# Attention scores and values in 64x64 tiles of TensorE, and the transposes moved behind a projection product

## The chip, the cores and the metric

The kernel runs on one core of one Trainium2 chip. A core has five engines with their own instruction queues: TensorE (PE, with its weight loads as PEld), VectorE (DVE), ScalarE (ACT), GpSimd (POOL) and SyncE (SP), which here only issues DMAs. They meet through semaphores. The metric is the device time of one execution in microseconds (us), the median of several runs.

## What is computed

Two layers over a sequence of 1024 rows of width 1024: an attention layer and a state-space layer, each followed by a residual and a layer norm. The change is in the attention layer alone. It has 16 heads of 64 columns and three groups of dilation (1, 4, 16). In each group a query sees keys within a window; the three results are merged by their softmax denominators.

```python
def _dilated_attention_mixer(h, w_in, w_out):
    proj = h @ w_in
    qkv = proj[..., :N_DIL * 3 * A_WIDTH].reshape(bsz, s, N_DIL, 3, A_HEADS, A_HEAD_DIM)
    gate = proj[..., N_DIL * 3 * A_WIDTH:]
    for g, (window, dil) in enumerate(((128, 1), (512, 4), (2048, 16))):
        o, l = _dilated_group(qkv[:, :, g, 0], qkv[:, :, g, 1], qkv[:, :, g, 2], window, dil, slopes)
    ...
    wts = softmax(stack(lses)); o = einsum('bshg,bshgd->bshd', wts, stack(outs))
    return (o.reshape(bsz, s, A_WIDTH) * silu(gate)) @ w_out
```

A group computes scores, adds a bias that falls with the distance, takes the exponential of the difference to the maximum, and multiplies with the values.

## The kernel before

The attention layer takes about the first 1,100 us. It works on two heads at a time, eight pairs in all; all pairs but the last run through the same code, the last has an order of its own (`last_pair`). The projections of a pair are ten tiles of 128 output columns, taken two at a time by a scheme with seven block products instead of eight. I call these products 0 to 6 of a unit. A product is 12 matmuls of 128x512 in `product` (L687) with weights w_f, the forms. There are seven forms a unit. ScalarE rounds each (`round_form`, L1046) and GpSimd subtracts to get its low part (`low_part`, L576). Product i can only begin when the low part of form i is there (w_ready). For forms 3 and 4 GpSimd must work in this order: raw form 3 (L605), low part 3, a difference (L608), raw form 4 (L612), low part 4.

The attention of a pair is cut into ten steps, d = 0 to 9: four of group 0, four of group 1 and two of group 2. A step has two units of `prob`, one for each head. An even step stands before products 0 to 3 and an odd step before products 4 to 6 of the same unit (`pair`, `stretch`, L944). In step d TensorE does

- the transposes of the probabilities of step d (`transpose_probs`, L766) into two banks of tp, which DVE copies to probT (`copy_t`, L1404),
- the values of step d-1 (`values`, L829 and L840) into the bank op, which ScalarE copies to num,
- in steps 0, 3 and 8 the transposes of V (L775), also through tp, and here the transposes of the probabilities stand behind the scores,
- the scores of step d+1 (`scores`, L756) into two banks of sp_.

DVE then takes the maxima of the scores with the bias (`tops`, L1384), ScalarE the exponentials (`softmax`, L1107). On ScalarE the softmax of step d+1 stands, in an even step, between the rounding of forms 2 and 3 (`even_step`). A product of float32 operands shows two records in the trace for each matmul of the program. Scores take 64 rows (a head) by 128 queries of the array, two heads beside each other; values 128 keys by 64 columns, again two beside each other.

The banks of tp are taken in turn by a list of events (`t_events`); an event can begin when the event two places before it has been copied (t_free). At the end of a pair, in step 9, the statistics (mz, the maxima and denominators) are transposed (L788) beside the sums for the next layer's constants (L782). DVE copies them to st, SP writes them to memory and reads them back as cz, and DVE computes differences (L1482 to L1485) and shares (L1491 to L1495) from them in the next step 0.

## Time and profile before

| | us |
|---|---|
| median of 3 runs | 2021.14 |
| lowest, highest | 2020.3, 2025.38 |
| the profiled execution | 2021.59 |
| its span | 2019.8 |
| TensorE busy | 1971.7 |
| GpSimd busy | 1267.8 |
| DVE busy | 1331.6 |
| ScalarE busy | 1060.8 |

The span is what the profile covers of the profiled execution, 1.8 us less than its time. Matmuls overlap, so the length of a matmul record says less than the distance of its start to the next one's. Where an engine sits idle, the profile says in brackets for how long and who ended it.

### The profile page before, as it was taken

To read this page: it belongs to the slowest core of one execution; us is meant where nothing else is said; L and a number is where in the kernel's file an instruction comes from. 1 tells how busy PE (TensorE), PEld (TensorE's weight loads), DVE (VectorE), ACT (ScalarE), POOL (GpSimd) and SP (SyncE) were. 2 spreads that over 40 slices of the span, in tenths; PEclk is the share of its full clock that TensorE was granted. 3 is DMA by queue.
4 is the path that set the end of the run, shared out by engine and by line. 5 is a ranking of instruction groups with operands and counts; after the bars stand their busy time and mean duration, and the time that the engine had idled before them with its cause. 6 is when DMAs were issued, how large, how long until landed. Compare 5 with 4: busy or idle time off the path is not lost.

```text
span 2019.8 us, 30446 instructions
## 1 busy us (share of the span) xinstructions
PE 1971.7 (98%) x10759; PEld 1569.4 (78%) x10759; DVE 1331.6 (66%) x2595; ACT 1060.8 (53%) x2578; POOL 1267.8 (63%) x841
## 2 busy tenths in 40 slices
PE   7999999999999999999999999899999999999998
PEld 4888877878888788777777867687787787777887
DVE  7547566475575664756647676798598598497553
ACT  5455455555545555545555254765665675675320
POOL 0566775867768667686584445376576576586572
PEclk8999999999999999999999999999999999999999
DMA  9112232222213222123234523465365365377531
GB/s 302 46 58 59 76 94 56 79 68 76 84 55 94 75 66 79 60 74 104 56 97 163 163 104 65 150 177 161 116 178 157 120 178 157 120 198 233 174 125 42
DMA packets 117590, 229.27 MB, mean 114 GB/s; under 512 B 22464, under 2 KB 55872, under 8 KB 117440
## 3 DMA queue, kind: packets, MB, share of 16 engines
q1 hardware_dynamic: 117440, 227.32, 37.2%
q8 instruction: 87, 1.43, 0.3%
q14 instruction: 63, 0.52, 0.1%
HBM read 199.42 MB, written 27.86 MB: 113 GB/s over the span
## 4 chain that ended last, share of the span: by engine, by line
PE 79%; DVE 9%; issue 3%; ACT 3%; POOL 2%; DMA 2%; SPq 2%; DVEq 0%; POOLq 0%; ACTq 0%
PE pp L687 27%; PE pp_s L2542 15%; PE po L687 10%; PE sp_ L756 4%; PE tp L766 4%; PE po L840 2%; DVE stage_s L3222 2%; PE pp_s L2746 2%; PE yo_p L2746 2%; PE po L829 2%; PE st_p L2559 1%; PE st_p L2746 1%; PE fill L2746 1%; DVE vv L3143 1%; PE yo_p L2574 1%
## 5 line engine op out<-in xcount | busy, mean ns | idle before, releaser
L687 PE MATMUL pp<-h_forms_hi,w_f 128*128 128x512 f32 x1576 | 516.7, 396 | 4.1 <-DVE temps L1432 2.6
L687 PEld LDWEIGHTS pp<-h_forms_hi,w_f 128*128 128x128 f32 x1576 | 296.2, 188 | 78.4 <-issue 12.0
L687 PE MATMUL pp<-h_forms_lo,w_f 128*128 128x512 f32 x788 | 307.6, 390 | 0.0
L576 POOL TENSOR_TENSOR w_f<-w_raw,w_f 128x512 fp32r<-128x512 f32 x154 | 199.3, 1314 | 161.4 <-ACT w_f L1046 161.4
L2542 PE MATMUL pp_s<-h_hi,w_hi_s 128*128 128x512 f32 x624 | 269.5, 432 | 5.3 <-DVE stage_s L3222 2.7
L1107 ACT ACTIVATE prob<-prob,mz 128x256 f32<-128x256 f32 (+2 forms) x384 | 169.9, 444 | 157.2 <-DVE mz L1384 157.0
L2542 PE MATMUL pp_s<-h_hi,w_lo_s 128*128 128x512 f32 x624 | 245.1, 393 | 0.0
L2542 PE MATMUL pp_s<-h_lo,w_hi_s 128*128 128x512 f32 x624 | 244.3, 391 | 0.0
L576 POOL TENSOR_TENSOR w_f<-w_f_raw,w_f 128x512 fp32r<-128x512 f32 x117 | 151.2, 1292 | 95.5 <-ACT w_f L1046 95.5
L687 PE MATMUL po<-h_forms_hi,w_f 128*128 128x512 f32 x632 | 209.4, 391 | 0.0
L687 PEld LDWEIGHTS pp<-h_forms_lo,w_f 128*128 128x128 f32 x788 | 148.3, 188 | 28.5
L2542 PEld LDWEIGHTS pp_s<-h_hi,w_hi_s 128*128 128x128 f32 x624 | 117.6, 188 | 48.9 <-issue 18.3
L3222 DVE SCALAR_TENSOR_TENSOR stage_s<-pp_s,gconv,stage_s 128x512 f32<-128x512 f32 (+2 forms) x184 | 137.9, 749 | 26.1 <-ACT stage_s L2816 20.6
L1046 ACT ACTIVATE w_f<-w_f_raw 128x512 fp32r<-128x512 f32 x118 | 74.4, 631 | 137.6 <-POOL w_f_raw L612 99.6
L2542 PEld LDWEIGHTS pp_s<-h_lo,w_hi_s 128*128 128x128 f32 x624 | 117.7, 189 | 31.2 <-issue 10.1
L2439 POOL TENSOR_TENSOR vv<-rw,vv 128x1024 f32<-128x1024 f32 x32 | 76.8, 2400 | 101.3 <-DVE vv L3143 98.6
L687 PEld LDWEIGHTS po<-h_forms_hi,w_f 128*128 128x128 f32 x632 | 118.9, 188 | 26.4 <-issue 1.8
L2141 POOL TENSOR_TENSOR w_lo_s<-w_raw_s,w_hi_s 128x1024 fp32r<-128x1024 f32 x40 | 100.0, 2500 | 62.3 <-ACT w_hi_s L2151 62.2
L2542 PEld LDWEIGHTS pp_s<-h_hi,w_lo_s 128*128 128x128 f32 x624 | 117.5, 188 | 26.3
L1384 DVE CUSTOM_DVE_ANT_0 prob<-sp_,bias,slope 128x256 f32<-128x256 f32 (+2 forms) x384 | 134.3, 406 | 3.9 <-PE sp_ L756 2.4
L1404 DVE COPY probT<-tp 128x512 f32<-128x512 f32 x160 | 102.8, 684 | 48.3 <-PE po L840 28.5
L1046 ACT ACTIVATE w_f<-w_raw 128x512 fp32r<-128x512 f32 x158 | 90.9, 622 | 63.9 <-PE pp L687 60.9
(568 smaller groups left out, 4407.1 us busy)
## 6 DMA issues: line engine op xcount, KB each, us to landing
w_raw<-in_a_w SPq DMA_DIRECT2D x80, 512.0 KB, 3.6
rw<-cum_rows SPq DMA_DIRECT2D x32, 1024.0 KB, 6.1
w_raw_s<-in_b_w SPq DMA_DIRECT2D x40, 512.0 KB, 4.6
ew<-exp_rows SPq DMA_DIRECT2D x64, 256.0 KB, 7.0
v<-in_ada_w SPq DMA_DIRECT2D x48, 256.0 KB, 3.0
qk<-merge_rows SPq DMA_DIRECT2D x42, 256.0 KB, 4.3
yT_b<-trunk SPq DMA_DIRECT2D x32, 256.0 KB, 2.6
stage_s<-yT_b SPq DMA_DIRECT2D x14, 512.0 KB, 4.7
```

What stands on the lines that cost most here:

```text
L576: return nc.gpsimd.tensor_tensor(out, x, hi.bitcast(F32), ALU.subtract)
L687: last = nc.tensor.matmul(bank, w[:, b], h[:, b], start=b == 0 and t == 0, stop=b == KS - 1 and t == 2)
L756: last = nc.tensor.matmul(sp_[:, h, c:c + w], q[rows, P * n:P * n + P], kT[g][rows, k0:k0 + w], start=True, stop=True)
L766: last = nc.tensor.transpose(tp[:, par, c * P:(c + 1) * P], prob[:, u % 2, c * P:(c + 1) * P], ident[:])
L1046: return nc.scalar.activation(dst, src, ACT.Copy, **kw)
L1107: last = nc.scalar.activation(prob[:, u % 2, c:c + w], prob[:, u % 2, c:c + w], ACT.Exp, scale=-1.0, bias=mz[:, m:m + 1], accum_out=mz[:, ...
L1384: last = nc.vector.tensor_tensor_reduce(out=prob[:, u % 2, c:c + w], in0=sp_[:, u % 2, c:c + w], in1=bias[:, c0:c0 + w], scale=slope[:, h: ...
L1404: nc.vector.tensor_copy(dst, src).then_inc(t_free, 2 if ev[0] == "e" else 1)
L2141: nc.gpsimd.tensor_tensor(flat(w_lo[:, slot]), flat(w_raw[:]), flat(w_hi[:, slot]).bitcast(F32), ALU.subtract).then_inc(S["lo_done"], 1)
L2542: last = nc.tensor.matmul(out, w[:, slot, k, :], of_h(h, k, half), start=(k == 0 and n == 0), stop=(k == KT - 1 and n == 2))
L2746: ins = nc.tensor.matmul(acc(m, half), y, w[:, half * HALF:(half + 1) * HALF], start=(k == 0 and i == 0), stop=(k == KO - 1 and i == 2))
L3222: ins = nc.vector.scalar_tensor_tensor(out, src[:, a - 2 + k - half * HALF:b - 2 + k - half * HALF], w[:, k:k + 1], out, ALU.mult, ALU.add)
```

## The change

Scores are computed in four 64x64 tiles: a head's 64 rows by 64 queries (twice as many matmuls). Values too: 64 keys by 64 columns. The two halves of the keys go to two banks, op and the bank of tp whose turn it is, so the list of events gets one more event x for each step. ScalarE copies the half in op to num, and DVE joins the half in tp to it (`join_values`); for step 0 the first half goes to a place in `spare` and is moved later (`first_values`). In group 1 the two tiles of scores are next to each other, so 3 blocks of probabilities are transposed and copied instead of 4, and a memset falls away. In group 2 only the 64 keys that a query can see are multiplied. In `pair` the values and the scores come first in a step, then the first product, and then the transposes of V, of the probabilities and of the statistics. The values of step 9 move into the next step 0. One sum of DVE (`sum_of_third`) moves behind the join, and ScalarE's copies of values stand earlier in their steps. The last pair's order is written anew, with the transposes still directly behind the scores.

```diff
 def score_columns(g, t):
-    return ((256 * t, 256), (320 * t, 192), (P * t, P))[g]
+    return ((256 * t, 256), (192 * t, 192), (P * t, P))[g]
+
+def blocks_of(g):
+
+    return (4, 3, 4)[g]
 def first_key(g, n):
     return (P * n, 256 * (n // 2) + 64 * (n % 2), P * n)[g]
...
         def t_events(early=False):
             out = []
             for d in range(DUOS):
+                if d:
+                    out += [("x", d - 1)]
                 v_events = [("v", V_AT[d], 0), ("v", V_AT[d], 1)] if d in V_AT else []
                 p_events = [("p", 2 * d), ("p", 2 * d + 1)]
                 out += p_events + v_events if d == 8 and early else v_events + p_events
...
                     else:
                         pe.wait_ge(pp_free, 4 * n - 2)
                     product(n, 0, b0)
+                    if after_first:
+                        after_first()
                     pe.wait_ge(w_ready, FORMS * n + 2)
                     if n == 1:
                         pe.wait_ge(pp_free, 1)
...
                     for t in range(nt):
                         n = n0 + t
                         k0, (c, w) = first_key(g, n), score_columns(g, t)
-                        for h in range(2):
-                            rows = slice(HD * h, HD * h + HD)
-                            last = nc.tensor.matmul(sp_[:, h, c:c + w],
-                                                    q[rows, P * n:P * n + P],
-                                                    kT[g][rows, k0:k0 + w], start=True, stop=True)
-                            if t == nt - 1:
-                                last.then_inc(s_full, 1)
+                        for part in range(2):
+                            cols = slice(HD * part, HD * part + HD)
+                            for h in range(2):
+                                rows = slice(HD * h, HD * h + HD)
+                                last = nc.tensor.matmul(sp_[cols, h, c:c + w],
+                                                        q[rows, P * n + HD * part:P * n + HD * part + HD],
+                                                        kT[g][rows, k0:k0 + w], start=True, stop=True)
+                                if t == nt - 1 and part == 1:
+                                    last.then_inc(s_full, 1)
                 def transpose_probs(j, u, at, par):
                     pe.wait_ge(p_ready, UNITS * j + (u + 1))
                     pe.wait_ge(t_free, T0 + at + 1)
-                    for c in range(4):
+                    for c in range(blocks_of(unit_of(u)[0])):
                         last = nc.tensor.transpose(tp[:, par, c * P:(c + 1) * P],
                                                    prob[:, u % 2, c * P:(c + 1) * P], ident[:])
                     last.then_inc(t_full, 1)
...
                                                         stop=(k == PAIRS - 1 and n == 2))
                     return last
-                def values(j, d, at):
+                def values(j, d, at, par):
                     g, n0, nt = duo_of(d)
-                    pe.wait_ge(t_free, T0 + at + 3)
-                    pe.wait_ge(o_free, DUOS * j + (d + 1))
-                    if g == 1:
-                        for i in range(2):
-                            for h in range(2):
-                                c = probT[:, h, :].rearrange("p (t i c) -> p i t c", t=2, i=2)
-                                last = nc.tensor.matmul(op[HD * h:HD * h + HD, 0:2 * P],
-                                                        v[g][:, n0 + i, HD * h:HD * h + HD], c[:, i],
-                                                        start=(i == 0), stop=(i == 1))
-                        last.then_inc(o_full, 1)
-                        return
-                    for t in range(nt):
-                        n = n0 + t
-                        keys = (n, (n + 1) % 8) if g == 0 else (n,)
-                        for i, kt in enumerate(keys):
-                            c = t * len(keys) + i
-                            for h in range(2):
-                                last = nc.tensor.matmul(
-                                    op[HD * h:HD * h + HD, t * P:(t + 1) * P],
-                                    v[g][:, kt, HD * h:HD * h + HD],
-                                    probT[:, h, c * P:(c + 1) * P],
-                                    start=(i == 0), stop=(i == len(keys) - 1))
-                    last.then_inc(o_full, 1)
+                    banks = (op, tp[:, par, :])
+                    pe.wait_ge(t_free, T0 + at + 2)
+                    if j or d:
+                        pe.wait_ge(first_half_in, DUOS * j + d)
+                    if g == 0:
+                        steps = [(t * P, P, (n0 + t + i) % 8, (t * 2 + i) * P, i == 0, i == 1)
+                                 for t in range(nt) for i in range(2)]
+                        steps = [(s, s) for s in steps]
+                    elif g == 1:
+
+                        steps = [((0, 2 * P, n0 + 1, P, True, False), (0, 2 * P, n0, 0, True, False)),
+                                 ((0, P, n0, 0, False, True), (P, P, n0 + 1, 2 * P, False, True))]
+                    else:
+                        steps = [tuple((t * HD, HD, n0 + t, t * P + HD * half, True, True) for half in range(2))
+                                 for t in range(nt)]
+                    for by_half in steps:
+                        for h in range(2):
+                            for half, (o0, w, kt, c0, first, final) in enumerate(by_half):
+                                keys = slice(HD * half, HD * half + HD)
+                                last = nc.tensor.matmul(banks[half][HD * h:HD * h + HD, o0:o0 + w],
+                                                        v[g][keys, kt, HD * h:HD * h + HD],
+                                                        probT[keys, h, c0:c0 + w], start=first, stop=final)
+                    last.then_inc(t_full, 1)
                 pe.wait_ge(ones_set, 2)
...
                         transpose_probs(j, u, NT * j + n, n % 2)
                 def duo_values(j, d, table):
-                    values(j, d, NT * j + table[("p", 2 * d + 1)])
-
-                def stretch(j, d, table):
-
-                    if d not in V_AT:
-                        new_probs(j, d, table)
+                    n = table[("x", d)]
+                    values(j, d, NT * j + n, n % 2)
+
+                def stretch(j, d, table, within=False):
+
                     if d:
                         duo_values(j, d - 1, table)
-                    new_v(j, d, table)
+                    elif j:
+                        duo_values(j - 1, DUOS - 1, T_AT)
                     if d < DUOS - 1:
                         scores(j, d + 1)
-                    if d in V_AT:
+                    else:
+                        scores(j + 1, 0)
+                    if not within:
+                        new_v(j, d, table)
                         new_probs(j, d, table)
                 def new_stats(j, table):
...
                     for d in range(DUOS):
                         n = 5 * j + (FIRST_UNITS + d // 2)
-                        stretch(j, d, T_AT)
-                        if d == DUOS - 1:
-                            scores(j + 1, 0)
-                            new_stats(j, T_AT)
-                            second_half(n, lambda: duo_values(j, DUOS - 1, T_AT))
-                        elif d % 2:
-                            second_half(n)
+                        stretch(j, d, T_AT, True)
+
+                        def transposes():
+                            new_v(j, d, T_AT)
+                            new_probs(j, d, T_AT)
+                            if d == DUOS - 1:
+                                new_stats(j, T_AT)
+
+                        if d % 2:
+                            second_half(n, transposes)
                         else:
-                            first_half(n)
+                            first_half(n, transposes)
                 def last_pair(j):
                     a, b, c = LAST_UNITS
...
                     g, h, n0, nt = unit_of(u)
                     dve.wait_ge(s_full, UNITS * j + (u + 1))
                     dve.sem_inc(tops_begun, 1)
-                    if u in (8, 9):
-
-                        nc.vector.memset(prob[:, u % 2, 192:320], 0.0)
                     for t in range(nt):
                         c0 = bias_columns(g, n0 + t)
                         m = stat_col(0, g, h, n0 + t)
...
                 def copy_t(ev, at, par, last_pair=False):
                     dve.wait_ge(t_full, at + 1)
                     if ev[0] == "p":
-                        dst, src = probT[:, ev[1] % 2, :], tp[:, par, :]
+                        w = P * blocks_of(unit_of(ev[1])[0])
+                        dst, src = probT[:, ev[1] % 2, 0:w], tp[:, par, 0:w]
                     elif ev[0] == "e":
                         dst, src = st[0:64], tp[0:64, par, 0:P]
                     elif ev[0] == "s" and last_pair:
...
                 def event(j, ev, table):
                     n = table[ev]
-                    if ev[0] == "p" and ev[1] % 2 == 0 and (ev[1] // 2 not in V_AT or ev[1] == 16 and table is T_LAST):
-                        dve.wait_ge(o_full, DUOS * j + ev[1] // 2)
                     copy_t(ev, T0 + NT * j + n, n % 2, table is T_LAST)
+
+                def join_values(j, d, table):
+
+                    g, n0, nt = duo_of(d)
+                    n = table[("x", d)]
+                    src = tp[:, n % 2, 0:2 * P]
+                    dve.wait_ge(t_full, T0 + NT * j + n + 1)
+                    if g < 2:
+                        dve.wait_ge(first_half_in, DUOS * j + d + 1)
+                        if d == 0:
+                            dst = first_place
+                        elif g == 0:
+                            dst = num[:, 0, :].rearrange("p (r n i) -> p r n i", r=16, n=8)[:, :, n0:n0 + 2]
+                            src = src.rearrange("p (n r i) -> p r n i", n=2, r=16)
+                        else:
+                            dst = num[:, 1, :].rearrange("p (a r b i) -> p a r b i", a=4, r=4, b=2)[:, :, d - 4]
+                            src = src.rearrange("p (b a i) -> p a b i", b=2, a=4)
+                        ins = nc.vector.tensor_tensor(dst, src, dst, ALU.add)
+                    else:
+                        dve.wait_ge(num_used, 3 * j + 3)
+                        if d == 9:
+                            dve.wait_ge(n_used, KT * j + IN_NUM)
+                        dst = num[:, 2, HALF * (d - 8):HALF * (d - 7)].rearrange("p (t s c) -> p s t c", t=4, s=2)[:, 1]
+                        ins = nc.vector.tensor_copy(dst, src.rearrange("p (t c) -> p t c", t=4))
+                    ins.then_inc(t_free, 1)
                 def silu(j, freed, half):
                     dve.wait_ge(pp_free, freed)
```

TensorE at steps 9 of a pair. L766 are transposes of probabilities, L840 values, L756 scores, L788 the transposed statistics, L782 sums, L687 product 4. Before:

```order
L766 MATMUL tp<-ident,prob 128x128 [waits t_free,p_ready]
...
L766 MATMUL tp<-ident,prob 128x128 [waits t_free,p_ready]
...
L840 MATMUL po<-probT,v12 64x128 [waits o_free,t_free]
L840 MATMUL po<-probT,v12 64x128 x7
L756 MATMUL sp_<-kT0,qT0 128x256 [waits s_free,pp_free]
L756 MATMUL sp_<-kT0,qT0 128x256 x3
L788 MATMUL tp<-ident,mz 128x128 [waits t_free]
L782 MATMUL tp<-ones,spare 128x1 [waits n_used]
...
L687 MATMUL pp<-h_forms_hi,w_f 128x512 [waits comb,w_ready]
```

After (L780, L856, L770, L802, L796 and L699 are the same things):

```order
L856 MATMUL po<-probT,v12 64x64 [waits first_half_in,t_free]
L856 MATMUL tp<-probT,v12 64x64
...
L770 MATMUL sp_<-kT0,qT0 64x256 [waits s_free,pp_free]
L770 MATMUL sp_<-kT0,qT0 64x256 x7
L699 MATMUL pp<-h_forms_hi,w_f 128x512 [waits comb,w_ready]
...
L780 MATMUL tp<-ident,prob 128x128 [waits t_free,p_ready]
L780 MATMUL tp<-ident,prob 128x128 x3
L780 MATMUL tp<-ident,prob 128x128 [waits t_free,p_ready]
L780 MATMUL tp<-ident,prob 128x128 x3
L802 MATMUL tp<-ident,mz 128x128 [waits t_free]
L796 MATMUL tp<-ones,spare 128x1 [waits n_used]
...
L699 MATMUL pp<-h_forms_hi,w_f 128x512 [waits pp_free,w_ready]
```

Probabilities and statistics moved from in front of product 4 (12 matmuls) to behind it.

TensorE at step 0, before (L775 is V, L687 the beginning of product 0):

```order
L775 MATMUL tp<-ident,vT 128x128 [waits t_free,pp_free]
...
L775 MATMUL tp<-ident,vT 128x128 [waits t_free,pp_free]
...
L756 MATMUL sp_<-kT0,qT0 128x256 [waits s_free]
L756 MATMUL sp_<-kT0,qT0 128x256 x3
L766 MATMUL tp<-ident,prob 128x128 [waits t_free,p_ready]
...
L766 MATMUL tp<-ident,prob 128x128 [waits t_free,p_ready]
...
L687 MATMUL pp<-h_forms_hi,w_f 128x512 [waits pp_free,w_ready]
```

And after; the first L699 is the beginning of product 0, the last that of product 1:

```order
L856 MATMUL po<-probT,v12 64x64 [waits first_half_in,t_free]
L856 MATMUL tp<-probT,v12 64x64
...
L770 MATMUL sp_<-kT0,qT0 64x256 [waits s_free]
L770 MATMUL sp_<-kT0,qT0 64x256 x7
L699 MATMUL pp<-h_forms_hi,w_f 128x512 [waits pp_free,w_ready]
...
L789 MATMUL tp<-ident,vT 128x128 [waits t_free,pp_free]
...
L789 MATMUL tp<-ident,vT 128x128 [waits t_free,pp_free]
...
L780 MATMUL tp<-ident,prob 128x128 [waits t_free,p_ready]
...
L780 MATMUL tp<-ident,prob 128x128 [waits t_free,p_ready]
...
L699 MATMUL pp<-h_forms_hi,w_f 128x512 [waits pp_free,w_ready]
```

The values of step 9 came in at the front, and all transposes moved behind product 0.

DVE in the same place after the change: differences, the sum of product 6, the join, V copies, shares, copies of probabilities and the first maximum.

```order
L1535 TENSOR_TENSOR cm<-cz 32x64 [waits cz_in]
L1536 TENSOR_TENSOR cm<-cm,cz 32x64 [waits v_step1]
L1538 TENSOR_TENSOR cz<-cz,cm 32x192 [waits v_step1]
L1507 TENSOR_TENSOR po<-po,temps 128x512 [waits comb,pp_full]
L1461 COPY num<-tp 128x4x64 [waits n_used,num_used,t_full]
L1433 COPY v0<-tp 128x512 [waits t_full] x2
L1544 TENSOR_TENSOR cz<-cz 32x192 [waits ce_ready]
...
L1548 TENSOR_TENSOR cz<-cz,cm 32x192 [waits v_step1]
L1433 COPY probT<-tp 128x512 [waits t_full] x2
L1412 ISA prob,mz<-sp_,bias,slope 128x256 [waits s_full]
```

Only the row L1461, the join, is new in this sequence; the rest stands as before.

## Rows read from the trace of the kernel before

**Rows 1.** The page: busy time of the engines; the chain that ended last.

```profile
PE 1971.7 (98%) x10759; PEld 1569.4 (78%) x10759; DVE 1331.6 (66%) x2595; ACT 1060.8 (53%) x2578; POOL 1267.8 (63%) x841
...
PE 79%; DVE 9%; issue 3%; ACT 3%; POOL 2%; DMA 2%; SPq 2%; DVEq 0%; POOLq 0%; ACTq 0%
```

**Rows 2.** TensorE's waits from 200 to 1100 us: in total, times, longest.

```profile
PE pp L687 <- DVE temps L1432: 2.6, 3, 0.9
PE pp L687 <- POOL w_f L576: 1.4, 2, 0.8
```

**Rows 3.** Time line of TensorE in step 2: start, length, instruction, count.

```profile
495.10 1.03 PE L766 MATMUL tp<-ident,prob 128*128 128x128 f32 x8
496.07 1.09 PE L840 MATMUL po<-probT,v 128*64 128x128 f32 x16
497.09 1.13 PE L756 MATMUL sp_<-kT,qT 64*128 64x256 f32 x8
498.16 0.50 PE L687 MATMUL pp<-h_forms_hi,w_f 128*128 128x512 f32 x1
498.50 0.39 PE L687 MATMUL pp<-h_forms_lo,w_f 128*128 128x512 f32 x1
```

**Rows 4.** Time line of TensorE in step 3, one with V transposes.

```profile
509.27 1.09 PE L840 MATMUL po<-probT,v 128*64 128x128 f32 x16
...
511.31 0.92 PE L756 MATMUL sp_<-kT,qT 64*128 64x192 f32 x8
512.16 1.09 PE L766 MATMUL tp<-ident,prob 128*128 128x128 f32 x8
513.01 0.47 PE L687 MATMUL pp<-h_forms_hi,w_f 128*128 128x512 f32 x1
```

**Rows 5.** Line 859, four column tiles: time line; durations (min, median, max ns).

```profile
9.36 1.06 PE L859 MATMUL tp<-num,bias 128*32 128x512 f32 x8 [0.45 <-DMA num<-in_ada_w]
...
L859 PE MATMUL tp<-num,bias x8: 592/604/617, 9.4 to 9.8; 128*32 128x512 f32 x8
```

**Rows 6.** Time lines of GpSimd and TensorE before product 3 of a step 0.

```profile
349.17 1.27 POOL L576 TENSOR_TENSOR w_f<-w_f_raw,w_f 128x512 fp32r<-128x512 f32 x1 [3.52 <-ACT w_f L1046]
...
350.49 0.50 PE L687 MATMUL pp<-h_forms_hi,w_f 128*128 128x512 f32 x1 [0.84 <-POOL w_f L576]
```

**Rows 7.** Time lines from one step 0 to the next and its product 3.

```profile
469.79 0.38 PE L775 MATMUL tp<-ident,vT 128*128 128x128 f32 x2
...
590.81 0.29 DVE L1404 COPY st<-tp 96x128 f32<-96x128 f32 x1 [0.81 <-PE tp L782]
...
598.41 0.21 DVE L1482 TENSOR_TENSOR cm<-cz 32x64 f32<-32x64 f32 x1 [0.57 <-DMA cz<-stats]
...
600.19 1.03 PE L775 MATMUL tp<-ident,vT 128*128 128x128 f32 x8
...
606.41 0.46 DVE L1384 CUSTOM_DVE_ANT_0 prob<-sp_,bias,slope 128x256 f32<-128x256 f32 x1
...
610.01 1.29 POOL L576 TENSOR_TENSOR w_f<-w_f_raw,w_f 128x512 fp32r<-128x512 f32 x1 [2.49 <-ACT w_f L1046]
...
611.36 0.50 PE L687 MATMUL pp<-h_forms_hi,w_f 128*128 128x512 f32 x1
```

**Rows 8.** Time lines of three engines in step 8.

```profile
571.60 0.44 PE L829 MATMUL po<-probT,v 128*64 128x256 f32 x2
...
576.63 0.34 DVE L1384 CUSTOM_DVE_ANT_0 prob<-sp_,bias,slope 128x128 f32<-128x128 f32 x1
...
581.63 1.29 POOL L576 TENSOR_TENSOR w_f<-w_f_raw,w_f 128x512 fp32r<-128x512 f32 x1 [1.59 <-ACT w_f L1046]
...
586.73 1.28 POOL L576 TENSOR_TENSOR w_f<-w_f_raw,w_f 128x512 fp32r<-128x512 f32 x1 [0.74 <-ACT w_f L1046]
```

**Rows 9.** Time line of TensorE at its longest wait.

```profile
1187.30 0.47 PE L2542 MATMUL pp_s<-h_hi,w_hi_s 128*128 128x512 f32 x1 [2.44 <-DVE h_lo L2183]
```

**Rows 10.** Stretches: length; busy of PE, PEld, DVE, ACT, POOL; granted clock; DMA.

```profile
1188.00:1190.00 2.00, 2.00 (x7) 1.53 (x6) 2.00 (x4) 1.17 (x3) 0.00 (x0) 0.57 0.36 147
```

172 lines of the change are left out of this document (96 added, 76 removed).

## The prediction

> **What bounds the kernel now.** I read first the page's busy shares and chain, then the list of waits, then time lines of single steps. TensorE is busy 98% of the span and carries 79% of the chain that ended last [rows 1]. In the attention part, from 200 to 1100 us, the two largest waits of its projection products come to 4.0 us, in five places [rows 2]. So every microsecond of TensorE's own work taken away there is worth one microsecond, as long as nobody else becomes late. The reader should next ask how late the others may be. The answer is in the first idle gap: at 350.49 TensorE stood 0.84 us for GpSimd's w_f, just after a low part that ran from 349.17 to 350.44 [rows 6]. That is product 3 of step 0, and 261 us (two pairs of heads) later the same product starts at 611.36 while the low part it needs ends at 610.01 + 1.29 = 611.30 [rows 7]. The margin at this place is zero in one pair and negative in another. Whatever delays this low part costs its full length.
>
> **What TensorE saves.** A product is 12 matmuls, 0.228 us apart, 2.74 us. I count the lengths by starts, not by busy time.
>
> Mode changes. A step without V transposes: transposes at 495.10, values at 496.07, scores at 497.09, product at 498.16 and its second matmul at 498.50 [rows 3]. From 495.10 to 498.50, less one product matmul, is 3.17 us. Scores of 256 columns take 1.07 us, those of 192 columns 0.85 [rows 3, 4], so 8 records stream 64 columns in 0.215: 8 records of 256, and 16 of 128 as well, stream for 0.86. Eight transposes stream for about 0.87 (0.85 from 512.16 to 513.01, and the product behind them begins a little early). That is 2.59 in this step. The rest, 0.58 us, is three changes of the tile's form. A step with V transposes takes 509.27 to 513.01, plus 0.09 before and 0.09 behind it (the second product matmul comes late there too), 3.92 us, of which 0.68 is not streaming (0.86 + 0.87 + 0.64 + 0.87 are) [rows 4]. Afterwards values and scores have one form (64 rows by 64 columns) and the transposes have the products' form, so a step has two changes: 0.14 into the values (a drain and a short weight load) and 0.20 into the product (a drain and a load of 128 columns), 0.34 together. Seven steps save 0.2, three save about 0.3, and the last step's values no longer stand alone between two products: 2.2 us a pair of heads in all. By the Trainium skill ("TensorEngine Tiling (Array Packing)", Key Properties) a change of tiling mode, not of tile, drains the engine; the trace agrees: values and scores take 0.16 to 0.21 us more than they stream, and the transposes in front of a product do not.
>
> Streaming. Twice as many matmuls of half the rows or columns, four beside each other instead of two, take the same time, if the four do run together. Four column tiles do: 8 records of 512 columns, each of 0.59 to 0.62 us, took 1.06 us together [rows 5]. Two column tiles do as well: the first two records of the values at 571.60 are over in 0.44 us [rows 8]. Four tiles of 64 by 64 are nowhere in the trace. Bounds: like two at a time, +14.8 us a pair; like four, +0. The 14.8 is what values (7.0) and scores (7.8) stream in a pair. I take four, because that row is the nearest in number of tiles. Less work is streamed in three places a pair: group 1 has 3 transposes instead of 4 in 8 units (8 x 0.109 = 0.87), its values read 256 and 128 columns instead of 256 and 256 (4 steps x 0.21 = 0.85), and group 2's values read only the half of the keys that matters (2 steps x 0.42 = 0.84). Together 2.56. With the mode changes: **4.75 us a pair**, out of 130.4 (469.79 to 600.19 in [rows 7]).
>
> DVE gets a join of the two halves of the values in each step, 128x256. It has no row; the nearest, copies of 128x512 at 0.64, bound it at 0.3 to 0.7, 10 a pair. DVE has the room (busy 66% of the span [rows 1]) and what it loses at two memsets and shorter copies it gets back. The price is that the second half takes a bank of tp and that the join stands ahead of the copies.
>
> **What becomes late.** The transposes of the probabilities of step d, which stood before the scores, now stand behind the next product. DVE's order is copies of these first, then the maxima of the new scores, then ScalarE's softmax, and only behind that on ScalarE the rounding of form 3, GpSimd's low part 3, two differences, and low part 4. Products 3 and 4 wait for these low parts. So first maxima, softmax and everything behind move by about 3 us, and TensorE arrives no later. I walk it with t = 0 at a step's first attention instruction.
>
> Step 0 of a pair (seven of them, from the second pair on). Before: the statistics are copied at 590.81, come back from memory at 598.41 (7.6 us), DVE works without a pause until the maxima start at 606.41 (8.0 us: differences, sum, V copies, shares, probT copies), and low part 3 ends at 611.30 (4.9 us) [rows 7]. That is 20.5 us, and TensorE's own program between the same points is six products (16.4) and 4.1 of steps, also 20.5. Afterwards the statistics are transposed behind product 4, so only five products (13.7) and step 0 (3.45: values 0.62, scores 0.86, changes 0.2, 16 transposes 1.75) stand between, 17.1 less 0.1. DVE's chain is 20.5 + 0.4 for the join. Stall: 20.9 - 17.0 = 3.9, say **4.0 us** with the bank waits below inside it. In the first pair, without shares, 1.1.
>
> Step 8. Before: values at 571.60, first maximum at 576.63, low part 3 ends at 581.63 + 1.29, low part 4 at 586.73 + 1.28 [rows 8]: 6.3 and 11.4 us behind the first maximum. Afterwards: scores over and product 0 begun at 1.77, over at 4.62, V transposes until 5.5. The first transposes of the probabilities need the bank of the first V half, which is copied at 4.62 + 0.33 + 0.31 + 0.65 = 5.9; the second wait likewise until 6.6; both together end 0.7 us late. The copies end at 7.85, low part 3 at 14.15, product 3 could begin at 12.6: 1.55. Low part 4 at 19.2 against 14.2 + 2.74 + 1.6 = 18.5: 0.7. Together **2.95 us**.
>
> The other steps. Step 2: product 0 over at 4.84, copies over at 6.7, low part 3 at 6.7 + 4.9 = 11.6, product 3 due at 1.99 + 0.11 + 8.21 + 0.87 = 11.2, and a little at product 4: 0.55. Steps 4, 6 and 7 are the same sum with shorter maxima: I take 0.5 each. Step 3 has the V bank wait of 0.7; step 9 waits 0.45 for the copy of the first probabilities before the statistics. Together **3.3 us** (bounds 0 and 8, since each is a difference of two sums of 11 to 16 us). All waits: 10.2 us a pair, 5.5 more than is saved.
>
> Clock. After TensorE had stood idle for 2.44 us before 1187.30 [rows 9] the granted clock was 0.57 from 1188 to 1190 [rows 10], that is 1.2 GHz for most of it. The wait before product 3 in step 0 will be about 3 us. A fall costs a little under the 2 us that such a stretch lasts, say 1.7. I take it in under half of seven cases, 5 us; bounds 0 and 15.
>
> Sum, against the profiled execution's own 2021.6: seven whole pairs, -33.3 (7 x 4.75) + 43.4 (7 x 6.2, steps 2 to 9) + 28.0 (7 x 4.0) + 1.1, the last pair, which is laid out otherwise and where three waits of 0.88 sit now, -3 (bounds -8 and +6), clock +5: +41.2, 2062.8. The median is 0.5 lower: **2062 us**.
>
> **Rivals.** (a) The waits are hidden and the gain stays. Then 8 x 4.75 = 38 off: 1983; with step 0 alone stalling, 2012. For it: TensorE hardly waits now, and steps 2, 4 and 6 come out within half a microsecond of no wait. Against it: step 0 has no margin [rows 6, 7] and its chain is lengthened by one product less the transposes. It decides at a sum of waits under 4.75 us a pair. Chance 0.13.
> (b) The waits are as told, but smaller by half, 5.1 a pair: 2020 to 2035. Chance 0.10.
> (c) As forecast, 2035 to 2100. Chance 0.68.
> (d) The four tiles don't run together, or a row pair and a column pair exclude each other: 14.8 us more a pair, of which the waits take little back: 2150 to 2180. For it: no row shows such tiles; the second passes of a float32 matmul must also find their turn. 
> (e) The change of place does not do what it says: each step would still have three changes; 8 x 2.2 = 17.6 us are then missing: 2080. Chance 0.03, inside (c)'s range.
>
> **How the numbers follow.** The likeliest case gives 2062. Two in ten may be left out: (a) with 0.13 below and (d) with 0.06 above. From the bounds of the small waits (0 to 8 a pair, that is -23 to +33), of the clock and of the last pair, not all at once: 2022 to 2105. A difference of 0.3% (6 us) is about what a measurement of this kernel tells from none; faster than 2015: 0.13; within: 0.05; slower: 0.82.
>
> **What would show it.** TensorE's idle time for POOL w_f rises from a few us to over 50 in the attention part, most of it before product 3 of step 0 (one gap of 3 us per pair) and of step 8. The first maximum of step 0 starts 16 us after the statistics' copy, as before, but product 3 is by then due. Changes: from values to scores no gap; 32 records of values in about 0.87 us. A pair of heads lasts about 136 us instead of 130.4. It would be wrong if ScalarE reaches form 3 before the softmax, if the statistics return much faster than 7.6 us, or if values of 16 tiles take 1.7 us instead of 0.9, which is (d).

## The result, and the profile after

The changed kernel takes 2074.84 us (median of 4 runs, 2072.96 to 2077.05) against 2020.72 for the kernel before in the same comparison (4 runs). The ratio is 1.0265, 95% interval 1.0244 to 1.0286. The profiled execution took 2075.57 us, its span is 2073.7. That is 54.0 us more than the profiled execution before; +41.2 was forecast.

The page of the changed kernel, answering [rows 1]: busy time of the engines, and the chain that ended last.

```profile
PE 1970.5 (95%) x12487; PEld 1549.4 (75%) x12487; DVE 1309.3 (63%) x2659; ACT 1040.6 (50%) x2586; POOL 1260.2 (61%) x841
...
PE 42%; POOL 20%; DVE 13%; issue 12%; ACT 9%; DMA 3%; SPq 1%; DVEq 0%; POOLq 0%; ACTq 0%
```

TensorE's busy time fell by only 1.2 us although it has less to stream, and its share of the chain fell from 79% to 42%. POOL, issue time, ACT and DVE took the difference: the page's list by line now has the low parts (POOL w_f L584) with 8% and the softmax (ACT prob L1129) with 3% on the path.

TensorE's waits from 200 to 1100 us (total, times, longest), answering [rows 2]:

```profile
PE pp L699 <- POOL w_f L584: 41.1, 36, 3.9
PE tp L780 <- DVE v L1433: 8.3, 19, 0.4
PE tp L789 <- DVE num L1461: 2.7, 1, 2.7
```

How long a pair of heads lasts can be read from the first and last transpose of statistics, one for each of seven pairs. From the kernel before, then from the changed one (start of the first, start of the last):

```profile
L788 PE MATMUL tp<-ident,mz x7: 329/329/329, 197.4 to 981.8; 128*128 128x128 f32 x7
```

```profile
L802 PE MATMUL tp<-ident,mz x7: 329/329/333, 202.7 to 1041.0; 128*128 128x128 f32 x7
```

Six pairs last 784.4 and 838.3 us, so 130.7 and 139.7 each (136 forecast). They make +53.9. The beginning up to the first mark makes +5.3, all behind the last mark -5.3: the last pair, which keeps its transposes behind the scores, and what follows.

**Step 0.** Time line of DVE in the changed kernel at a pair's beginning, answering [rows 7]: copy of the statistics, first difference after they came back, V copies, the first of the shares, copies of probabilities, first maximum.

```profile
482.54 0.29 DVE L1433 COPY st<-tp 96x128 f32<-96x128 f32 x1 [0.62 <-PE tp L796]
...
489.58 0.33 DVE L1535 TENSOR_TENSOR cm<-cz 32x64 f32<-32x64 f32 x1 [2.55 <-DMA cz<-stats]
...
492.99 1.29 DVE L1433 COPY v<-tp 128x512 f32<-128x512 f32 x2 [1.51 <-PE tp L789]
494.19 0.40 DVE L1544 TENSOR_TENSOR cz<-cz 32x192 f32<-32x192 f32 x1
...
497.95 1.27 DVE L1433 COPY probT<-tp 128x512 f32<-128x512 f32 x2
499.15 0.46 DVE L1412 CUSTOM_DVE_ANT_0 prob<-sp_,bias,slope 128x256 f32<-128x256 f32 x1
```

The trip through memory takes 7.0 us (7.6 before). From the return to the first maximum it is 9.6 us instead of 8.0, because DVE stood idle for 1.51 us: the V transposes now stand behind product 0. Then GpSimd's low part 3, and TensorE behind it:

```profile
502.74 1.26 POOL L584 TENSOR_TENSOR w_f<-w_f_raw,w_f 128x512 fp32r<-128x512 f32 x1 [5.74 <-ACT w_f L1068]
```

```profile
500.14 0.39 PE L699 MATMUL po<-h_forms_hi,w_f 128*128 128x512 f32 x1
504.05 0.80 PE L699 MATMUL pp<-h_forms_hi,w_f 128*128 128x512 f32 x1 [3.53 <-POOL w_f L584]
...
509.47 0.47 PE L856 MATMUL po<-probT,v 64*64 64x128 f32 x1
```

Two things are to be seen. Product 3 waits 3.53 us. And then it takes from 504.05 to 509.47, 5.42 us, where a product takes 2.74 and 0.1 for the change to the values. The windows (length, busy time, granted clock, DMA share and GB/s) give the reason: a clock at 0.50 of full speed, the level of 1.2 GHz, from about 503.2, before the wait was over, until 510:

```profile
502.00:504.00 2.00, 0.00 (x0) 0.79 1.05 238
504.00:506.00 2.00, 1.95 (x5) 0.50 0.60 131
506.00:508.00 2.00, 2.00 (x6) 0.50 0.20 33
508.00:510.00 2.00, 2.00 (x16) 0.50 0.63 229
510.00:512.00 2.00, 2.00 (x46) 1.00 0.00 0
```

By the same starts product 3 of step 0 takes 5.42 us in five pairs and 4.26 in the first of six. In that first pair the clock was still 1.00 when the product began at 225.32 and stood at 0.50 only from about 226.7 to 230.

**Steps 2, 7, 8.** Time line of TensorE in the changed kernel. Step 2 (answers [rows 3]), then the waits before product 4 in step 7 and before products 0 and 3 in step 8:

```profile
520.57 0.39 PE L699 MATMUL po<-h_forms_hi,w_f 128*128 128x512 f32 x1
520.89 0.32 PE L856 MATMUL po<-probT,v 64*64 64x128 f32 x1
520.90 0.32 PE L856 MATMUL tp<-probT,v 64*64 64x128 f32 x1
520.90 0.32 PE L856 MATMUL po<-probT,v 64*64 64x128 f32 x1
520.91 0.32 PE L856 MATMUL tp<-probT,v 64*64 64x128 f32 x1
...
521.82 1.04 PE L770 MATMUL sp_<-kT,qT 64*64 64x256 f32 x16
522.79 0.50 PE L699 MATMUL pp<-h_forms_hi,w_f 128*128 128x512 f32 x1
523.12 0.40 PE L699 MATMUL pp<-h_forms_lo,w_f 128*128 128x512 f32 x1
...
525.64 1.03 PE L780 MATMUL tp<-ident,prob 128*128 128x128 f32 x8
526.43 0.48 PE L699 MATMUL pp<-h_forms_hi,w_f 128*128 128x512 f32 x1
526.75 0.40 PE L699 MATMUL pp<-h_forms_lo,w_f 128*128 128x512 f32 x1
...
588.34 0.50 PE L699 MATMUL pp<-h_forms_hi,w_f 128*128 128x512 f32 x1 [0.67 <-POOL w_f L584]
...
599.75 0.50 PE L699 MATMUL pp<-h_forms_hi,w_f 128*128 128x512 f32 x1 [0.59 <-POOL w_f L584]
...
612.30 0.50 PE L699 MATMUL pp<-h_forms_hi,w_f 128*128 128x512 f32 x1 [1.48 <-POOL w_f L584]
```

Four 64x64 tiles start within 0.02 us of each other and 32 records are through in 0.93 us (520.89 to 521.82). So they do run beside each other, and case (d) of the rivals is out. By the Trainium skill ("TensorE: Matmul & The Clock Gate", Measured speedup vs the span model) packs of tiles run beside each other with a few ns a tile; the trace agrees, with 7 ns between starts.

### The profile page after: what moved, and what is told of

Same layout as the page of the kernel before. It is cut to its first block, busy times and chain, and to the rows that moved or that the text cites. A ratio compares the mean times of both kernels' runs of the same rounds, so it can differ in the third digit from the quotient of the medians.

```text
span 2073.7 us, 34018 instructions
## 1 busy us (share of the span) xinstructions
PE 1970.5 (95%) x12487; PEld 1549.4 (75%) x12487; DVE 1309.3 (63%) x2659; ACT 1040.6 (50%) x2586; POOL 1260.2 (61%) x841
## 4 chain that ended last, share of the span: by engine, by line
PE 42%; POOL 20%; DVE 13%; issue 12%; ACT 9%; DMA 3%; SPq 1%; DVEq 0%; POOLq 0%; ACTq 0%
PE pp_s L2601 13%; PE pp L699 10%; POOL w_f L584 8%; ACT prob L1129 3%; POOL w_f_raw L603 2%; POOL w_f_raw L613 2%; DVE stage_s L3281 2%; PE yo_p L2805 2%; PE pp_s L2805 2%; POOL w_raw L605 2%; ACT w_f L1068 2%; POOL w_f_raw L620 1%; PE st_p L2618 1%; POOL w_raw L616 1%; PE st_p L2805 1%
## 5 line engine op out<-in xcount | busy, mean ns | idle before, releaser
L699 PE MATMUL pp<-h_forms_hi,w_f 128*128 128x512 f32 x1576 | 548.2, 410 | 45.4 <-POOL w_f L584 44.4
L699 PEld LDWEIGHTS pp<-h_forms_hi,w_f 128*128 128x128 f32 x1576 | 302.1, 192 | 142.8 <-POOL w_f L584 74.3
L1129 ACT ACTIVATE prob<-prob,mz 128x256 f32<-128x256 f32 (+2 forms) x384 | 170.0, 444 | 353.6 <-DVE mz L1412 353.6
L584 POOL TENSOR_TENSOR w_f<-w_raw,w_f 128x512 fp32r<-128x512 f32 x154 | 203.1, 1336 | 192.5 <-ACT w_f L1068 190.7
L699 PE MATMUL pp<-h_forms_lo,w_f 128*128 128x512 f32 x788 | 314.2, 399 | 0.0
L584 POOL TENSOR_TENSOR w_f<-w_f_raw,w_f 128x512 fp32r<-128x512 f32 x117 | 151.7, 1297 | 149.9 <-ACT w_f L1068 149.9
L699 PE MATMUL po<-h_forms_hi,w_f 128*128 128x512 f32 x632 | 208.2, 389 | 0.0
L1433 DVE COPY probT<-tp 128x512 f32<-128x512 f32 (+1 forms) x160 | 94.6, 631 | 144.3 <-PE tp L780 144.1
L699 PEld LDWEIGHTS pp<-h_forms_lo,w_f 128*128 128x128 f32 x788 | 151.7, 192 | 25.9
L699 PEld LDWEIGHTS po<-h_forms_hi,w_f 128*128 128x128 f32 x632 | 118.6, 188 | 24.6
L1484 DVE TENSOR_TENSOR temps<-pp,temps 128x512 f32<-128x512 f32 x39 | 27.0, 691 | 167.1 <-PE pp L699 167.1
```

The costliest lines, as they stand in the source:

```text
L584: return nc.gpsimd.tensor_tensor(out, x, hi.bitcast(F32), ALU.subtract)
L699: last = nc.tensor.matmul(bank, w[:, b], h[:, b], start=b == 0 and t == 0, stop=b == KS - 1 and t == 2)
L1129: last = nc.scalar.activation(prob[:, u % 2, c:c + w], prob[:, u % 2, c:c + w], ACT.Exp, scale=-1.0, bias=mz[:, m:m + 1], accum_out=mz[:, ...
L1433: nc.vector.tensor_copy(dst, src).then_inc(t_free, 2 if ev[0] == "e" else 1)
```

## Experiments: tiles and placement apart

Each kernel does the whole computation. All ratios are against the kernel before, run on the same chip.

**tiles_only** takes the placement back and keeps the tiles.

```diff
+                        early = True
+                        if early:
+                            transposes()
                         if d % 2:
-                            second_half(n, transposes)
+                            second_half(n, None if early else transposes)
                         else:
-                            first_half(n, transposes)
+                            first_half(n, None if early else transposes)
```

> The changed kernel with one thing undone: in every step of the seven whole pairs the transposes (V, probabilities, statistics) stand again directly behind the scores, ahead of the product. The 64x64 tiles, the join on DVE and the two banks stay. Theory (the placement loses, the tiles gain): a pair of heads lasts about 2.6 us less than the 130.4 of the kernel before, less about 1 us where the join of 0.4 us lengthens DVE's chain in steps 0 and 8, so 128.5 to 129; the whole about 2005 to 2012, and the wait before product 3 of step 0 is under 1 us. Rival (the tiles themselves lose: twice as many instructions, the join in front of the copies, a bank of tp less): 2040 or more, with waits for DVE all over the pair.

Measured: 2035.13 us, ratio 1.0058 (1.0042 to 1.0075). Neither theory held. The wait in step 0 went as expected, but the tiles, without the placement, are no gain either. The waits of this kernel from 200 to 1100 us, and TensorE and DVE in step 6 (DVE: three rows of the next layer's constants, the sum of product 6, the join):

```profile
PE tp L780 <- DVE num L1458: 13.2, 7, 2.2
PE tp L789 <- DVE num L1458: 9.1, 6, 1.5
```

```profile
557.60 0.52 PE L780 MATMUL tp<-ident,prob 128*128 128x128 f32 x3 [2.16 <-DVE num L1458]
```

```profile
552.15 1.01 DVE L1570 TENSOR_SCALAR spare<-v,cond 128x512 f32<-128x512 f32 x1
553.28 1.57 DVE L1573 SCALAR_TENSOR_TENSOR spare<-v,cond,spare 128x512 f32<-128x512 f32 x1
554.96 1.56 DVE L1573 SCALAR_TENSOR_TENSOR spare<-num,cond,spare 128x512 f32<-128x512 f32 x1
556.44 0.69 DVE L1510 TENSOR_TENSOR po<-po,temps 128x512 f32<-128x512 f32 x1
557.04 0.41 DVE L1458 TENSOR_TENSOR num<-tp,num 128x256 f32<-128x256 f32 x1
```

The values' second half lies in a bank of tp, and the second four or three transposes need that bank. The join that frees it stands behind 4.1 us of rows of constants and one sum. In the changed kernel a product of 2.74 us stands between values and transposes and covers the join. This is a use of the placement that the prediction did not see: it named the bank of tp as a price, but put the join into the sum as DVE time only.

**place_only** is the kernel before, old tiles, with the placement alone (the values of step 9 stay behind product 5).

```diff
-                        stretch(j, d, T_AT)
+                        if d:
+                            duo_values(j, d - 1, T_AT)
+                        if d < DUOS - 1:
+                            scores(j, d + 1)
+                        else:
+                            scores(j + 1, 0)
...
-                            first_half(n)
+                            first_half(n, None, None, transposes)
```

> The kernel before with the placement alone: scores and values in the old tiles, but in every step of the seven whole pairs the values and scores first, then the first product, then the transposes. The values of step 9 stay behind product 5. Theory: the mode changes save at most 2.2 us a pair, the waits cost about 10 and the slower clock behind the wait of step 0 about 2.8, so some 10 us more a pair and 2080 to 2100 in all. Rival (the tiles make the loss): 2015 to 2025.

Measured: 2120.47 us, ratio 1.0472 (1.0455 to 1.0489). The placement makes the loss, in the old tiles too; it was larger than the 2080 to 2100 expected. Its waits, 200 to 1100 us:

```profile
PE pp L687 <- POOL w_f L576: 39.6, 32, 4.6
PE po L842 <- ACT num L1058: 9.8, 6, 1.6
```

The first row is nearly that of the changed kernel. The second was not foreseen: the values of step 1, at 542.16, wait 1.63 us for ScalarE's copy of those of step 0 (541.60), which stands in its old place behind the softmax and three other copies. The changed kernel has these copies earlier in their steps, so this kernel is not the placement alone. A pair lasts 145.5 us, 5.8 more than in the changed kernel; 1.6 of it is this wait, and most of the rest is, by estimate, the 4.4 that TensorE's own steps save with the tiles (counted below).

**rows_spread** is tiles_only with those rows of DVE spread, to see whether the tiles gain once the join is in time.

```diff
-                NEXT_AT = {5: (0, 1, 2), 6: (3, 4, 5), 7: (6, 7)}
+                NEXT_AT = {5: (1,), 6: (3, 4, 5), 7: (7,)}
+                EARLY_AT = {5: (0,), 6: (2,), 7: (6,)}
...
-                            first_sums(n, lambda: next_rows(j, d))
+                            first_sums(n, lambda: next_rows(j, d), lambda: weigh_next(j, EARLY_AT.get(d, ())))
```

> tiles_only (transposes directly behind the scores in all steps of the whole pairs) with one edit: the eight rows for the next layer's constants, which DVE works off as 3 in step 5, 3 in step 6 and 2 in step 7, stand as 1+1, 1+3 and 1+1, those of the first number in a gap of DVE between two sums. In tiles_only TensorE waited 2.2 us in step 6 and 1.5 in step 8 for the join of the values, which stood behind 4.1 and 3.0 us of such rows. Theory (the join has no cover once the transposes follow the scores at once, and these rows are what makes it late): both waits go, 132.6 us a pair become 128 to 129 and the whole 2004 to 2012, below the kernel before. Rival (the join waits for ScalarE's half of the copy, not for the rows): over 2025.

Measured: 2006.73 us, ratio 0.9917 (0.9896 to 0.9939), faster than the kernel before. Both waits went. What is left from 200 to 1100 us is mostly the V banks, 0.2 to 0.6 us a time:

```profile
PE tp L780 <- DVE v L1436: 7.6, 20, 0.6
```

**before_rows** gives the kernel before the same spread rows.

> The kernel before, old tiles and old order, with only the rows for the next layer's constants spread as in rows_spread. Theory (the join is what these rows held up, and the kernel before has none): no change, 2018 to 2026, so that what rows_spread gained over the kernel before belongs to the 64x64 tiles. Rival (the rows cost the kernel before something too): 2005 to 2015.

Measured: 2020.73 us, ratio 0.9996 (0.9986 to 1.0005). The rows cost the kernel before nothing, so the 0.8% of rows_spread belongs to the tiles.

## Experiments: what product 3 waits for, and the clock

**product_twice** adds work in the wait: product 2 is computed twice in step 0 of six pairs.

```diff
+                    if twice:
+                        product(n, 2, b2, counted=False)
                     product(n, 2, b2)
...
-                            first_half(n, transposes)
+                            first_half(n, transposes, twice=d == 0 and j > 0)
```

> The changed kernel with work added: in step 0 of the pairs 1 to 6 product 2 is computed twice into its bank, 12 more matmuls (2.74 us) just before the wait of 3.5 to 3.9 us in front of product 3. The result is the same. Theory (the wait lowers TensorE's clock, and product 3 then takes 5.1 us instead of 2.7): the added work hides in the wait, the idle time left is about 0.9, the granted clock stays 1.0 and the kernel gets faster by 2.6 us for each of six pairs, to 2058 to 2062. Rival (the slow product 3 has another reason, such as DMA traffic beside it): product 3 stays slow and the time at 2075.

Measured: 2061.43 us, ratio 1.0183 (1.0168 to 1.0199), 0.8% less than the changed kernel with 72 more matmuls. A pair lasts 137.2 us (205.2 to 1028.2 for six) instead of 139.7. TensorE's time line at product 3, and the windows:

```profile
502.24 0.50 PE L699 MATMUL pp<-h_forms_hi,w_f 128*128 128x512 f32 x1 [0.96 <-POOL w_f L584]
...
505.19 0.32 PE L858 MATMUL po<-probT,v 64*64 64x128 f32 x1
```

```profile
500.00:502.00 2.00, 1.27 (x6) 1.00 1.00 234
502.00:504.00 2.00, 1.76 (x8) 1.00 0.60 133
```

Product 3 takes 2.95 us instead of 5.42, at a full clock and with the DMA as busy beside it (0.60 from 502 to 504; 0.60, 0.20 and 0.63 beside the slow product). So the slow product was the clock, and the clock was the idle time before it.

Shorter waits are less certain. In tiles_only TensorE stands for 2.16 us in the same place of six pairs, ending at 292.33, 424.97, 557.60, 690.23, 822.89 and 957.80. The windows behind the third and the fifth:

```profile
558.00:560.00 2.00, 2.00 (x11) 1.00 0.25 92
```

```profile
823.00:825.00 2.00, 2.00 (x7) 0.50 0.34 117
```

Five of the six kept their clock. The pair with the fall lasted 134.3 us, the four before it 132.6 each.

**stats_early** puts only step 9 back: its transposes stand ahead of product 4.

```diff
+                        early = d == DUOS - 1
+                        if early:
+                            transposes()
...
```

> The changed kernel, but in step 9 alone the transposes of probabilities and statistics stand again ahead of product 4. Theory (the trip of the statistics through memory starts one product too late): it starts 2.7 us earlier, the wait of 3.6 before product 3 of step 0 falls to about 1 and the clock no longer falls, which was 2.7 more; 5 to 6 us less for each of six pairs: 2038 to 2046. Rival (in step 0 it is product 0 ahead of the V transposes that holds DVE up, which stood idle for 1.5 us before the V copies): the wait stays over 2 us and the time over 2060.

Measured: 2045.53 us, ratio 1.0112 (1.0094 to 1.013). A pair lasts 135.2 us instead of 139.7. The wait before product 3 is 1.67 in five of the six pairs and the clock does not fall; in the sixth it is 2.00, and there it does:

```profile
L802 PE MATMUL tp<-ident,mz x7: 329/329/329, 199.5 to 1011.0; 128*128 128x128 f32 x7
```

```profile
492.85 0.50 PE L699 MATMUL pp<-h_forms_hi,w_f 128*128 128x512 f32 x1 [1.67 <-POOL w_f L584]
```

**early09** puts step 0 back as well (`early = d in (0, DUOS - 1)`).

> The changed kernel with steps 0 and 9 in the old place (transposes directly behind the scores), the other eight steps as changed. Theory (with the statistics early, the 1.67 us still waited before product 3 of step 0 come from step 0's own product standing ahead of its transposes, for which DVE stood idle): that wait and the 0.44 for the V bank go, some 2 us of the 134.9 of stats_early a pair, 2030 to 2036 in all. What then remains over rows_spread is what the placement costs in steps 1 to 8. Rival (the trip through memory alone sets it): the wait stays over 1 us and the time at 2042 or more.

Measured: 2034.88 us, ratio 1.0069 (1.0052 to 1.0085). The wait before product 3 is gone. So two products make the stall: the one that the statistics stand behind, and the one that the V transposes stand behind, for which DVE was idle. The prediction had the first alone. The pair of this kernel (198.9 to 998.1, 133.2 each) against that of rows_spread (198.2 to 972.5, 129.1 each) bounds what the placement costs in steps 1 to 8. It is a bound only, because rows_spread also has the rows in their new places:

```profile
L802 PE MATMUL tp<-ident,mz x7: 328/329/329, 198.9 to 998.1; 128*128 128x128 f32 x7
```

```profile
L802 PE MATMUL tp<-ident,mz x7: 328/330/330, 198.2 to 972.5; 128*128 128x128 f32 x7
```

**form3_first** leaves the placement and cuts the chain behind the maxima on ScalarE.

```diff
+                    round_form(n, 3)
                     softmax_of()
-                    round_form(n, 3)
```

> The changed kernel, but on ScalarE in every even step the rounding of form 3 stands ahead of the softmax instead of behind it. Theory (what product 3 waits for is low part 3, which waits for the softmax, which waits for maxima that the placement made late): form 3 is rounded at once when its raw form is there, low part 3 ends long before product 3 is due, and what is left in step 0 is the copy of product 0's bank on DVE, which stands behind the maxima too: about 1 us instead of 3.6, with no fall of the clock, and nothing or little in step 8 instead of 1.5. Some 7 us less a pair, 2025 to 2035. Rival (DVE's chain is what ends last, the low part only the last sign of it): the wait in step 0 stays above 2 us, the clock still falls and the time is over 2055.

Measured: 2028.28 us, ratio 1.0029 (1.0019 to 1.004): some 47 us less than the changed kernel (2.3%) from one line of order. TensorE's waits, 200 to 1150 us:

```profile
PE pp L699 <- POOL w_f L584: 7.7, 12, 0.7
PE pp L699 <- DVE temps L1476: 7.2, 6, 1.6
```

The low parts fall from 41.1 to 7.7 us. In their place stands what was hidden behind them, DVE's copy of product 0's bank, 1.2 us in each of six pairs.

**form3_copy_first** also puts that copy ahead of the copies of the probabilities.

```diff
+                    def begin_next():
+                        shares(ch, j)
+                        first_copy(5 * j + (FIRST_UNITS + 5))
...
```

> As form3_first, and on DVE the copy of product 0's bank (which frees it for product 3) stands ahead of the copies of the probabilities in every even step. Theory: product 3 then waits for nothing behind the maxima; 1 us a pair less than form3_first, 2018 to 2028, and the waits left are those for banks of tp (0.44, three a pair) and for form 4 and form 0 in steps 7 and 8 (0.7, 0.6). Rival: the copy ahead pushes the maxima back by 0.7 and the later low parts with them, no gain over form3_first.

Measured: 2022.18 us, ratio 1.0 (0.9989 to 1.0011). The copy's wait is gone; the whole loss of the change is given back by two edits of order.

**chain_cut** adds the early statistics, and on ScalarE form 4 ahead of the projection tile.

```diff
+                    round_form(n, 4)
                     first_tile(j, n, kinds, 0)
-                    round_form(n, 4)
```

> form3_copy_first with two edits more: the statistics of step 9 are transposed ahead of product 4 (as in stats_early), and on ScalarE form 4 is rounded ahead of the copy of the projection tile. Theory: the chain from the statistics to the maxima of step 0 has its 2.7 us back, low part 4 is in time in step 7, a pair lasts 129 to 130 us and the whole 2005 to 2012, under the kernel before. Rival (something else, such as ScalarE's own work, then ends last): 2020 or more.

Measured: 2012.45 us, ratio 0.995 (0.9935 to 0.9965), faster than the kernel before, and just above the 2005 to 2012 expected. What is left in a pair of 130.2 us (199.4 to 980.8 for six) are three V banks of 0.44, one of 0.35 for the statistics and the waits of steps 7 and 8. That of step 7 stayed at 0.7, so the edit for form 4 did not do what I meant it for; why was not followed up.

**rows_form3** puts the two edits on ScalarE into rows_spread.

> rows_spread with ScalarE's form 3 rounded ahead of the softmax and form 4 ahead of the copy of the projection tile. Theory (with the transposes directly behind the scores no low part is late, and what is left are waits for banks of tp): no change against rows_spread beyond 2 us, 2004 to 2008. Rival (low parts still cost something there): 2000 or less.

Measured: 2003.74 us, ratio 0.9913 (0.9899 to 0.9928), the same as rows_spread within the intervals. With the transposes directly behind the scores no low part is late. The best kernel with the placement, chain_cut, stays 0.4% above it.

## Why the prediction was right, and where it was off

The direction, the mechanism and the range (2022 to 2105) held. +41.2 was forecast, +54.0 measured. I count a pair (481 to 621 us) by starts, each step's clean length apart from its waits, against the pair of the kernel before from 459.25 to 589.65. The two differ by 9.4 us (139.8 and 130.4).

| us a pair | forecast | counted |
|---|---|---|
| TensorE's own steps | -4.75 | -4.4 |
| step 0: V bank, product 3 | 4.0 | 0.8 + 3.7 |
| step 8: V bank, products 3 and 4 | 2.95 | 0.8 + 1.7 + 0.2 |
| other steps | 3.3 | 3.7 |
| clock | 0.7 | 2.8 |
| sum | 6.2 | 9.3 |

- **The clock was the mis-sized term.** 5 us were forecast for it in all, bounds 0 and 15: a fall in under half of seven cases, at 1.7 each. It fell in all six pairs, at 2.6 us of product 3 and 0.2 of the values behind it (1.4 and 0.2 in the first): some 16 us. It fell once more behind a wait of 2.70 in the last pair, where it stood at 0.50 for about 3.4 us, by estimate another 1.7 us. That makes about 17, above the upper bound. The step that failed is the reading of [rows 9, 10]: the length of one slow window of 2 us was taken as the length of a fall, although the next window of the same trace has the same clock:

```profile
1190.00:1192.00 2.00, 2.00 (x7) 1.56 (x6) 2.00 (x5) 0.00 (x0) 0.00 (x0) 0.57 0.00 0
```

Two windows at 0.57 are about 3.4 us at 0.50, so 1.7 us of work lost; 2 us at half speed would lose only 1. The 1.7 for a fall of that kind was thus a wrong reading with a fitting number, which is luck. In five of the six pairs the clock stayed low for about 6.8 us, 503.2 to 510 here, and the whole product ran in it. product_twice shows this by itself: 2.5 us a pair back.
- **TensorE's savings were right but for a few tenths.** Step 2 takes 2.97 us (520.80 to 522.79, 0.10 at the second matmul, 525.64 to 526.43, 0.09) against 3.17, so 0.20 saved as forecast. Over the ten steps it is 0.7, 0.2, 0.25, 0.2, 0.3, 0.6, 0.5, 0.7, 0.35 and 0.6. But the saving comes from the tiles and from values and scores standing together. Behind a product the transposes still cost 0.09 us at the next one, so the placement itself saves next to nothing: steps without a wait last 11.13 us (step 1) and 13.60 (step 4) in rows_spread, without it, and 11.17 and 13.47 in chain_cut, with it.
- **The waits were right in sum, 10.2 against 10.9, and in place.** Step 0 was right partly for a wrong reason. The trip was shorter than forecast (7.0 for 7.6), and DVE's part longer (9.6 for 8.0 and 0.4 for the join), since the V transposes had moved behind product 0; early09 shows that part by itself. Step 8's 1.55 measured 1.48, the 0.7 for product 4 only 0.2. The wait of 0.6 before product 0 of step 8 was missing from the forecast. The sign "over 50" us of idle time for POOL w_f was set too high: it is 41.1 from 200 to 1100 us and 44.4 in the whole kernel.
- **The join** was costed as 0.3 to 0.7 us of DVE and is that (0.40). That TensorE needs its bank next, so that a late join stops the transposes, and that the product in between covers it, was not priced. It does not touch this forecast, but without it the change cannot be understood: its alternative, tiles_only, is slower than the kernel before as well.
- **First and last pair.** The beginning cost 5.3 us where the sum had 2.5 (6.2 + 1.1 - 4.75). Everything behind the last mark gave 5.3 back where the sum had 1.0 more (4.0 - 3). Together these misses are 3.5 us below the sum and hide a part of the clock's.
- **Sums.** Two small ones don't close: the mode changes listed come to 2.3 us before the last step's values are added, where 2.2 was entered, and the other steps' waits to 3.2, where 3.3 was. Neither moves the total by more than 1 us.
- **Rivals.** (a) and (b) fall with 10.9 us of waits a pair, where (a) needed under 4.75 and (b) had 5.1; (d) with the tile starts; (e) is half right: three changes became two, but not through the placement.

## What to carry to other kernels

When work is moved behind a long instruction group to give its inputs time, walk the chain that starts at the moved work: here every consumer of the transposes, up to the low parts of the next weights, moved with them. Look first for a queue in which an urgent short task stands behind a late long one; exchanging two lines on ScalarE was worth some 47 us, more than all that the tiles could gain. An idle stretch of TensorE is to be priced with the slow work behind it, and a bank that a new result occupies is a new wait even where its engine has time.

## What the runs showed of the hardware

- 12 matmuls of work put into a wait of 3.5 us made each pair 2.5 us shorter, through the clock alone.
- After waits of 3.53 to 3.86 us the granted clock stood at 0.50 for about 6.8 us, in five pairs; it had fallen before the wait was over. After a wait of 3.49 us it stood there for about 3.4 us only and fell 1.4 us after work had begun again.
- It also fell, for about 3.4 us each, after 2.70 us in the last pair and after 2.00 us once (stats_early); after the same 2.16 us (tiles_only) it fell in one pair and not in five others, and after 1.67 us (stats_early) not in five pairs. So the price of a wait near 2 us is not the same from one pair to the next.
- Four 64x64 tiles of float32 run beside each other: starts about 7 ns apart, and 32 records of 128 columns through in 0.93 us, where 16 of them in two tiles took 1.02 before (496.07 to 497.09 in [rows 3]).
- In the chain of step 0 two short operations of DVE took 1.2 us each (L1545 and L1546 in the changed kernel), where operations on the same 32x64 took 0.21 in the kernel before (L1492 and L1493) and in chain_cut. Both ended about 0.1 us after a low part or a raw form of GpSimd beside them. The kernel before has two such operations in this chain as well (L1483, L1491), so they are in both of its lengths, 8.0 and 9.6 us. The cause was not tested.
